# Three-term products of a split-precision linear: the order of the matmuls in a granule, and one wait less

## The chip, the cores and the metric

The kernel runs on one core of a Trainium2 chip. The metric is the time of one execution on the device, in microseconds. Engines by their names in the profile: PE is TensorE (PEld its loads of stationary tiles), DVE is VectorE, ACT is ScalarE, POOL is GpSimd, SP is the engine that issues the weight transfers.

## The reference

A forward pass over 256 tokens with a model width of 2048: two blocks (the first with stick-breaking attention and a gated delta rule, the second with block attention and dilated attention, each followed by a gated feed-forward layer of width 5632), then a block with causal pooling and a state-space mixer. Cut to what matters here, nearly all of the arithmetic is products of a 256-row activation with a large float32 weight:

```python
proj = u @ w_in                                    # 2048 x 7184, 2048 x 6144, 2048 x 4096
u = mixed @ w_out                                  # 2048 x 2048
u = (jax.nn.silu(u @ w_gate) * (u @ w_up)) @ w_down   # 2048 x 5632, twice, and back
```

## The kernel before

**Split products.** Both operands of each such product are split in two numbers of a shorter format (fp32r): x = xh + xl and w = whi + wlo. The result is the sum of three products, xh·whi + xl·whi + xh·wlo, accumulated in float32. The activations are split once for each linear (`xh`, `xl`, and `hTh`, `hTl` for the hidden layer). The weights are split as they arrive.

**Granules.** A linear (`ev_gdn`, `ev_sb`, `ev_z`, `ev_out`, `up0a`, ..., `pg`, 19 of them in this order) is cut in chunks of 512 output columns, and a chunk in granules. A granule is 2 tiles of 128 rows of the weight by 512 columns. There are 948 of them in the kernel, numbered from 0; `s_in` begins with granule 800. The 256 tokens are two tiles (t = 0, 1), so that a granule has 2 (rows j) x 2 (tokens t) x 3 (products) = 12 matmuls of 128x128 by 128x512. The x slice is the stationary operand, the weight slice the moving one. A chunk accumulates in a pair of PSUM banks, one for each t, and successive chunks take the two pairs in turn.

**The ring.** SP brings raw weights, two granules a transfer. For each granule ScalarE copies raw to `whi` (L1020, counted by the semaphore `hi_done`), VectorE subtracts to get `wlo` (L1621, counted by `lo_done`). Both go to one of four places (RING = 4). TensorE counts `used` after the last matmul of a granule, and ScalarE writes the place for granule g only when `used` is at g - 3. SP waits for `lo_done` before it brings the next weights to a raw place:

```python
act.wait_ge(S("used"), g - (RING - 1))                       # ScalarE, L1019
act.activation(whi[:, place % RING], raw_granule(place), ACT.Copy).then_inc(S("hi_done"), 1)
dve.wait_ge(S("hi_done"), g + 1)                             # VectorE, L1620
```

**Order of the other work.** Each engine has one program written out by hand. On TensorE small jobs (transposes, attention, the delta rule, the state-space part) stand between two granules (`aside`). On ScalarE and VectorE they stand between two splits, in one queue with them, so that a split can be late because of what stands before it. At the start of a linear the new activation is transposed on TensorE (L524), and split by ScalarE and VectorE, during the first three granules. The split of the fourth granule's weights stands behind that. In `s_in` VectorE has, for each of 8 column tiles, rotations (`pc<-side,grow`), scans (L2210) and products (`u<-u,grow`), with weight splits between them; TensorE has for each the input products L904 and four output groups L914 to L917, two of them before the second granule after the products, two after. A product of VectorE waits for an earlier output group (`y_part`), because its result goes to one of two places that the group reads.

The function that the change touches stands below, with what calls it. `granules` walks through a linear, and `hidden` does the same for the gate and up products of the feed-forward layer in a loop.

Of the kernel before, what the change touches and what calls it, by code (L numbers as in the profile page):

```python
# [14 lines left out]
P = 128  # L15
TOK = 256
TT = TOK // P
# [99 lines left out]
def build(nc, A, out):  # L117

    ctx = ExitStack()
    with ctx:  # L120
        def sb(name, shape, dt=F32, scope=ctx):
            return scope.enter_context(nc.sbuf_tensor(name, [P] + shape, dt))
# [3 lines left out]
        whi = sb("whi", [RING, 2, CH], F32R)  # L126
        wlo = sb("wlo", [RING, 2, CH], F32R)
# [29 lines left out]
        acc = [ctx.enter_context(nc.psum_tensor(f"acc{i}", [P, CH], F32)) for i in range(4)]  # L157
# [22 lines left out]
        def S(name):  # L180

            if name not in sems:
                sems[name] = ctx.enter_context(nc.semaphore(name))
            return sems[name]
# [193 lines left out]
        def g16(k):  # L378

            return grow[:, 544 + 16 * k:560 + 16 * k]  # L380
# [10 lines left out]
        def unit(t, k):  # L391

            o = UNIT + (8 * t + k) * CH
            return ar[:, o:o + CH].rearrange("p (h n) -> p h n", h=4)
# [52 lines left out]
        def _(pe):  # L447
# [8 lines left out]

            def granule(g, ring, pair, lhs_h, lhs_l, k0, first, last):

                def sweep(x, w, start=False, stop=False):
                    for j in range(2):  # L460
                        for t in range(TT):
                            mm = pe.matmul(acc[2 * pair + t][:], x[:, k0 + j, t * P:t * P + P], w[:, ring, j],  # L462
                                           start=start and j == 0, stop=stop and j == 1)
                    return mm

                pe.wait_ge(S("hi_done"), g + 1)
                sweep(lhs_h, whi, start=first)
                sweep(lhs_l, whi)
                pe.wait_ge(S("lo_done"), g + 1)
                sweep(lhs_h, wlo, stop=last).then_inc(S("used"), 1)  # L470

            def linear(*args):
                for _ in granules(*args):
# [2 lines left out]
            def granules(name, lhs_h, lhs_l, freed, aside=None, first_use=None):  # L476

                per = KTS[name] // 2  # L480
                for c in range(CHUNKS[name]):
                    pair = (CHUNK0[name] + c) % 2
                    for j in range(per):
                        if aside:
                            aside(c, j)
                        if first_use:
                            first_use(c, j)
                        if j == 0:
                            for t in range(TT):
                                claim(acc[2 * pair + t], *freed(c, t))  # L490
                        g = gran(name, c, j)
                        granule(g, g % RING, pair, lhs_h, lhs_l, 2 * j, j == 0, j == per - 1)
                        yield
# [168 lines left out]
            for hg in range(2):  # L662
                for t in range(TT):
                    n = 2 * hg + t

                    for s, (o, ready) in enumerate(((1024, "kT_ready"), (0, "qT_ready"))):
                        b = claim(side[2 * t + s], "kT_done" if s == 0 else "qT_done", n + 1)
                        for k in range(4):
                            c0 = o + (4 * hg + k) * P
                            mm = pe.transpose(b[:, k * P:k * P + P], qkv[:, t, c0:c0 + P], ident)  # L670
                        mm.then_inc(S(ready), 1)
                beside()
                for t in range(TT):

                    b = claim(side[2 * t], "decay_arg", 9 * (2 * hg + t + 1))
                    for k in range(4):
                        c0 = t * 8 + 4 * hg + k
                        mm = pe.matmul(b[:, k * P:k * P + P], g16(GL)[:, c0:c0 + 1].to_broadcast([P, P]), tri_u,
                                       start=True, stop=True)
                    mm.then_inc(S("gb_ready"), 1)  # L680
                beside()
                for t in range(TT):
                    n = 2 * hg + t
# [8 lines left out]
                for t in range(TT):  # L692
                    n = 2 * hg + t
                    pe.wait_ge(S("L_done"), lower(n))
                    b = claim(side[2 * t + 1], "LT_done", n + 1)
                    for k in range(4):
                        mm = pe.transpose(b[:, k * P:k * P + P], unit(t, M_)[:, k], ident)
# [75 lines left out]
            def hidden(name):  # L773
                n0, blocks, g0 = FFB[name], CHUNKS[name] // 2, GRAN0[name]

                def block_of(i, first):
                    for m in range(2):
                        for j in range(8):
                            if m == 0 and j == 2 and not first:
                                pe.wait_ge(S("hTl_done"), 2 * n0 + 2 * i - 2)  # L780
                                turn_hidden(i + (n0 - 1))
                            if j == 0:
                                if first:
                                    for t in range(TT):
                                        claim(acc[2 * m + t], "sg_done", 0)
                                else:
                                    pe.wait_ge(S("hm_done" if m else "sg_done"), 2 * n0 + 2 * i)
                            if first and m == 0 and name[3] == "a":
                                features_use(name, h)(0, j)
                            granule(i * 16 + (g0 + 8 * m + j), j % RING, m, xh, xl, 2 * j, j == 0, j == 7)  # L790

                block_of(0, True)
                with pe.Fori(1, blocks) as i:
                    block_of(i, False)
                for t in range(TT):
                    last_reader[acc[t].name] = (S("sg_done"), 2 * (n0 + blocks))
                    last_reader[acc[2 + t].name] = (S("hm_done"), 2 * (n0 + blocks))
                for b in range(2):
                    last_reader[side[b].name] = (S("hTl_done"), 2 * (n0 + blocks - 1))
# [1622 lines left out]
```

## Time and profile before

| | |
|---|---|
| median of 3 runs | 3032.73 us (3031.87 to 3033.37) |
| profiled execution, its own time | 3031.87 us |
| its span | 3030.1 us |
| TensorE busy | 2924.2 us, 97% |
| TensorE's loads busy | 2403.3 us, 79% |
| VectorE busy | 1731.7 us, 57% |
| ScalarE busy | 1415.6 us, 47% |
| GpSimd busy | 74.0 us, 2% |
| weights and the like moved by DMA | 515.45 MB, mean 170 GB/s |

Read from top to bottom: the execution took its own time, of which the span is the part that the profiler saw between first and last instruction. The busy times are shares of the span. Matmuls are pipelined, so a busy TensorE may still have small waits within; the timeline and the table of waits show these.

### The profile page before, as it was taken

To read this page: it belongs to the slowest core of one execution; us is meant where nothing else is said; L and a number is where in the kernel's file an instruction comes from. 1 tells how busy PE (TensorE), PEld (TensorE's weight loads), DVE (VectorE), ACT (ScalarE), POOL (GpSimd) and SP (SyncE) were. 2 spreads that over 40 slices of the span, in tenths; PEclk is the share of its full clock that TensorE was granted. 3 is DMA by queue.
4 is the path that set the end of the run, shared out by engine and by line. 5 is a ranking of instruction groups with operands and counts; after the bars stand their busy time and mean duration, and the time that the engine had idled before them with its cause. 6 is when DMAs were issued, how large, how long until landed. Compare 5 with 4: busy or idle time off the path is not lost.

```text
span 3030.1 us, 34851 instructions
## 1 busy us (share of the span) xinstructions
PE 2924.2 (97%) x13709; PEld 2403.3 (79%) x13709; DVE 1731.7 (57%) x2222; ACT 1415.6 (47%) x1809; POOL 74.0 (2%) x66
## 2 busy tenths in 40 slices
PE   8999999999999999999999999999999999989998
PEld 7888877788888888878887788888888877556876
DVE  5875655644544454554445545544454569998545
ACT  5543375544444444454446444444444454444444
POOL 0000000000000000000000000000000002210000
PEclk9999999999999999999999999999999999999999
DMA  6532245565555555555552565555655554335443
GB/s 236 176 126 93 89 140 189 179 194 193 181 194 194 194 185 190 193 177 185 188 187 86 175 207 187 190 191 194 194 190 185 194 175 132 98 104 168 172 157 125
DMA packets 255293, 515.45 MB, mean 170 GB/s; under 512 B 8240, under 2 KB 8464, under 8 KB 254144
## 3 DMA queue, kind: packets, MB, share of 16 engines
q1 hardware_dynamic: 252896, 501.61, 50.0%
q0 software_dynamic: 2272, 12.10, 1.2%
q8 instruction: 87, 1.43, 0.2%
q14 instruction: 38, 0.31, 0.0%
HBM read 511.58 MB, written 2.10 MB: 170 GB/s over the span
## 4 chain that ended last, share of the span: by engine, by line
PE 87%; DVE 9%; ACT 2%; issue 2%; DMA 0%; SPq 0%; DVEq 0%; ACTq 0%
PE acc L462 80%; PE side L658 2%; DVE u L1609 2%; DVE u L2210 1%; DVE pc L1609 1%; ACT ar L1009 1%; DVE wlo L1621 1%; DVE ar L1609 1%; PE side L524 1%; PE side L769 1%; PE side L553 1%; DVE ar L1612 0%; ACT whi L1020 0%; DMA raw<-in_ev_w_in 0%; ACT L1009 0%
## 5 line engine op out<-in xcount | busy, mean ns | idle before, releaser
L1621 DVE TENSOR_TENSOR wlo<-raw,whi 128x1024 fp32r<-128x1024 f32 x948 | 1155.3, 1226 | 1114.3 <-ACT whi L1020 1113.5
L1020 ACT ACTIVATE whi<-raw 128x1024 fp32r<-128x1024 f32 x948 | 996.8, 1059 | 1201.3 <-PE acc L462 1199.7
L462 PE MATMUL acc<-whi,xh 128*128 128x512 f32 x3072 | 841.1, 396 | 10.9 <-ACT whi L1020 4.7
L462 PE MATMUL acc<-wlo,xh 128*128 128x512 f32 x3072 | 825.4, 391 | 22.6 <-DVE wlo L1621 22.6
L462 PE MATMUL acc<-whi,xl 128*128 128x512 f32 x3072 | 824.1, 390 | 0.0
L462 PEld LDWEIGHTS acc<-wlo,xh 128*128 128x128 f32 x3072 | 577.6, 188 | 146.7 <-DVE wlo L1621 26.0
L462 PEld LDWEIGHTS acc<-whi,xl 128*128 128x128 f32 x3072 | 578.5, 188 | 122.2
L462 PEld LDWEIGHTS acc<-whi,xh 128*128 128x128 f32 x3072 | 568.9, 189 | 132.7 <-issue 9.6
L462 PE MATMUL acc<-whi,hTh 128*128 128x512 f32 x720 | 194.2, 392 | 2.7 <-ACT u L1009 2.7
L462 PE MATMUL acc<-wlo,hTh 128*128 128x512 f32 x720 | 193.3, 391 | 0.0
L462 PE MATMUL acc<-whi,hTl 128*128 128x512 f32 x720 | 193.3, 390 | 0.0
L462 PEld LDWEIGHTS acc<-whi,hTh 128*128 128x128 f32 x720 | 135.7, 189 | 30.9 <-ACT u L1009 2.9
L462 PEld LDWEIGHTS acc<-wlo,hTh 128*128 128x128 f32 x720 | 135.7, 189 | 28.3
L462 PEld LDWEIGHTS acc<-whi,hTl 128*128 128x128 f32 x720 | 135.7, 189 | 28.3
L658 PE MATMUL side<-ar 128*128 128x128 f32 x720 | 86.6, 277 | 10.1 <-ACT h L1009 6.6
L658 PEld LDWEIGHTS side<-ar 128*128 128x128 f32 x720 | 84.7, 192 | 14.4 <-DVE ar L1609 4.7
L1009 ACT ACTIVATE ar<-side 128x512 f32<-128x512 f32 (+2 forms) x121 | 65.7, 572 | 54.3 <-PE side L553 36.5
L1009 ACT ACTIVATE ar<-ar 128x512 f32<-128x512 f32 (+2 forms) x58 | 31.8, 559 | 101.3 <-DVE ar L1612 82.1
L1009 ACT ACT_TABLE_LOAD x57 | 73.1, 1283 | 12.8 <-DVE cols L1666 6.1
L1609 DVE TENSOR_TENSOR u<-u,grow 128x512 f32<-128x512 f32 x88 | 56.5, 686 | 4.2 <-ACT ar L1009 1.5
L524 PE MATMUL side<-cc,h 128*128 128x128 f32 x192 | 33.0, 338 | 21.3 <-DVE h L1612 18.8
L1009 ACT ACTIVATE ar<-acc,st 128x512 f32<-128x512 f32 x56 | 35.4, 684 | 36.1 <-PE acc L462 34.5
(227 smaller groups left out, 1356.5 us busy)
## 6 DMA issues: line engine op xcount, KB each, us to landing
raw<-in_ffn_w_gate SPq DMA_DIRECT2D x88, 1024.0 KB, 5.1
raw<-in_ffn_w_up SPq DMA_DIRECT2D x88, 1024.0 KB, 5.1
raw<-in_ffn_w_down SPq DMA_DIRECT2D x88, 1024.0 KB, 5.0
raw<-in_ev_w_in SPq DMA_DIRECT2D x56, 1024.0 KB, 5.1
raw<-in_od_w_in SPq DMA_DIRECT2D x48, 1024.0 KB, 5.1
raw<-in_w_in SPq DMA_DIRECT2D x32, 1024.0 KB, 5.3
raw<-in_ev_w_out SPq DMA_DIRECT2D x16, 1024.0 KB, 5.0
raw<-in_od_w_out SPq DMA_DIRECT2D x16, 1024.0 KB, 5.0
```

The lines of the kernel that those rows point to most:

```text
L462: mm = pe.matmul(acc[2 * pair + t][:], x[:, k0 + j, t * P:t * P + P], w[:, ring, j], start=start and j == 0, stop=stop and j == 1)
L524: mm = pe.transpose(b[:, j * TOK + t * P:j * TOK + t * P + P], src[:, t, k * P:k * P + P], ident)
L553: mm = pe.transpose(b[:, jb * TOK + t * P:jb * TOK + t * P + P], pj[:, t, (2 * j + jb) * P:(2 * j + jb + 1) * P], ident)
L658: mm = pe.matmul(bank[:, k * P:k * P + P], lhs(k), rhs(k), start=True, stop=True)
L769: mm = pe.transpose(side[b][:, jb * TOK + t * P:jb * TOK + t * P + P], hm[:, t, (2 * b + jb) * P:(2 * b + jb + 1) * P], ident)
L1009: act.activation(o, i, f, **kw).then_inc(S(done), 1)
L1020: act.activation(whi[:, place % RING], raw_granule(place), ACT.Copy).then_inc(S("hi_done"), 1)
L1609: dve.tensor_tensor(o, a, b, op).then_inc(S(done), 1)
L1621: dve.tensor_tensor(wlo[:, place % RING], raw_granule(place), whi[:, place % RING].bitcast(F32), ALU.subtract).then_inc(S("lo_done"), 1)
L2210: dve.tensor_tensor_scan(x, magnitude(4 * ct + r), x, start(r, m), mult, add)\
```

## The change

Before, a granule went through three sweeps of four matmuls: xh with whi, xl with whi, and then, behind a wait for `lo_done`, xh with wlo. Within a sweep the two banks of the pair alternated. After, the granule waits for `lo_done` at its head (`wlo` is computed from `whi`, so that `hi_done` is implied and its wait is gone), and then makes all three products of one (j, t) in a row, in the order xh·whi, xh·wlo, xl·whi. Three matmuls in a row thus go to one bank, then three to the other. The number of matmuls, their operands, the first and last of an accumulation and the count `used` are as before.

```diff
             def granule(g, ring, pair, lhs_h, lhs_l, k0, first, last):
 
-                def sweep(x, w, start=False, stop=False):
-                    for j in range(2):
-                        for t in range(TT):
-                            mm = pe.matmul(acc[2 * pair + t][:], x[:, k0 + j, t * P:t * P + P], w[:, ring, j],
-                                           start=start and j == 0, stop=stop and j == 1)
-                    return mm
-
-                pe.wait_ge(S("hi_done"), g + 1)
-                sweep(lhs_h, whi, start=first)
-                sweep(lhs_l, whi)
                 pe.wait_ge(S("lo_done"), g + 1)
-                sweep(lhs_h, wlo, stop=last).then_inc(S("used"), 1)
+                for j in range(2):
+                    for t in range(TT):
+                        tok = slice(t * P, t * P + P)
+                        for n, (x, w) in enumerate(((lhs_h, whi), (lhs_h, wlo), (lhs_l, whi))):
+                            mm = pe.matmul(acc[2 * pair + t][:], x[:, k0 + j, tok], w[:, ring, j],
+                                           start=first and j == 0 and n == 0,
+                                           stop=last and j == 1 and n == 2)
+                mm.then_inc(S("used"), 1)
```

## Rows read from the trace of the kernel before

**Rows 1.** The page: busy time, share and count of each engine; granted clock in tenths
```profile
PE 2924.2 (97%) x13709; PEld 2403.3 (79%) x13709; DVE 1731.7 (57%) x2222; ACT 1415.6 (47%) x1809; POOL 74.0 (2%) x66
...
PEclk9999999999999999999999999999999999999999
```

**Rows 2.** The page: the chain that ended last, by engine, shares of the span
```profile
PE 87%; DVE 9%; ACT 2%; issue 2%; DMA 0%; SPq 0%; DVEq 0%; ACTq 0%
```

**Rows 3.** Timeline of a steady stretch: start, length, engine, line, operation, count, idle before
```profile
1005.63 1.07 PE L462 MATMUL acc<-whi,xh 128*128 128x512 f32 x4
...
1008.35 1.07 PE L462 MATMUL acc<-whi,xh 128*128 128x512 f32 x4
1008.55 1.06 ACT L1020 ACTIVATE whi<-raw 128x1024 fp32r<-128x1024 f32 x1 [1.60 <-PE acc L462]
...
1009.64 1.23 DVE L1621 TENSOR_TENSOR wlo<-raw,whi 128x1024 fp32r<-128x1024 f32 x1 [1.43 <-ACT whi L1020]
```

**Rows 4.** Table of waits: who waited for whom, us in total, times, longest
```profile
PE acc L462 <- DVE wlo L1621: 22.6, 8, 3.7
```

**Rows 5.** Timeline of TensorE, first and last of 48 matmuls of L588
```profile
36.90 0.28 PE L588 MATMUL side<-xh,wab_h 128*16 128x256 f32 x1
...
42.41 0.28 PE L588 MATMUL side<-xl,wab_h 128*16 128x256 f32 x1
```

**Rows 6.** Timeline at starts: up0a, od_out, ev_gdn's granule 31, pg
```profile
591.72 3.50 DVE L1621 TENSOR_TENSOR wlo<-raw,whi 128x1024 fp32r<-128x1024 f32 x3
...
592.17 1.07 PE L462 MATMUL acc<-whi,xh 128*128 128x512 f32 x4
...
1642.04 4.63 DVE L1621 TENSOR_TENSOR wlo<-raw,whi 128x1024 fp32r<-128x1024 f32 x4
...
1642.83 1.07 PE L462 MATMUL acc<-whi,xh 128*128 128x512 f32 x4
...
113.92 1.22 DVE L1621 TENSOR_TENSOR wlo<-raw,whi 128x1024 fp32r<-128x1024 f32 x1 [0.19 <-ACT whi L1020]
...
113.94 1.19 PE L462 MATMUL acc<-whi,xh 128*128 128x512 f32 x4
...
2928.79 3.50 DVE L1621 TENSOR_TENSOR wlo<-raw,whi 128x1024 fp32r<-128x1024 f32 x3 [10.33 <-ACT whi L1020]
...
2928.90 1.16 PE L462 MATMUL acc<-whi,xh 128*128 128x512 f32 x4 [2.21 <-ACT whi L1020]
```

**Rows 7.** Timeline around one stall of s_in
```profile
2581.47 1.22 DVE L1621 TENSOR_TENSOR wlo<-raw,whi 128x1024 fp32r<-128x1024 f32 x1
...
2582.75 1.20 PE L462 MATMUL acc<-wlo,xh 128*128 128x512 f32 x4 [1.80 <-DVE wlo L1621]
...
2584.04 0.59 PE L914 MATMUL side<-u,ar 128*32 128x256 f32 x2
...
2584.47 0.59 PE L915 MATMUL side<-u,ar 128*32 128x256 f32 x2
...
2585.02 2.35 DVE L1621 TENSOR_TENSOR wlo<-raw,whi 128x1024 fp32r<-128x1024 f32 x2
...
2587.29 2.49 DVE L1609 TENSOR_TENSOR u<-u,grow 128x512 f32<-128x512 f32 x4
```

**Rows 8.** Timeline of the preparation in s_in
```profile
2520.01 2.77 DVE L1621 TENSOR_TENSOR wlo<-raw,whi 128x1024 fp32r<-128x1024 f32 x2
...
2520.47 1.07 PE L462 MATMUL acc<-whi,xh 128*128 128x512 f32 x4
...
2527.55 1.09 PE L893 MATMUL side<-cc,ar 128*128 128x128 f32 x8 [0.56 <-DVE ar L1609]
```

**Rows 9.** Timeline, a later stall; windows, end of row: PEclk, DMA share, GB/s
```profile
2661.98 2.08 PE L462 MATMUL acc<-wlo,xh 128*128 128x512 f32 x4 [3.70 <-DVE wlo L1621]
...
2667.65 2.50 DVE L1609 TENSOR_TENSOR u<-u,grow 128x512 f32<-128x512 f32 x4 [1.04 <-PE side L917]
...
2643.00:2670.00 27.00, 23.30 (x102) 14.58 (x100) 25.48 (x56) 10.89 (x12) 6.77 (x5) 0.87 0.31 101
```

## The prediction

> **What bounds the kernel now.** I read the page first. TensorE is busy for 97% of the span at a granted clock of nearly full speed, and VectorE for 57% [rows 1]. The chain that ended last runs for 87% on TensorE and 9% on VectorE [rows 2]: outside a few stretches, a microsecond added to TensorE's queue is a microsecond of the end.
>
> Then the timeline of a steady stretch. A granule (12 matmuls) starts at 1005.63 and the next at 1008.35, so a granule takes 2.72 us, 227 ns a matmul; the load of the stationary tile lies under the matmul before it. When the granule ends, ScalarE starts a whi at 1008.55 and VectorE ends the wlo from it at 1009.64 + 1.22 = 1010.86, 2.51 us after the end of that granule [rows 3]. It is for the granule that starts three later (the ring has four places), at 1008.35 + 3 x 2.72 = 1016.5. So in steady state wlo is ready some 5.6 us before its granule even starts. The table of waits agrees: in the whole kernel, the matmuls waited for wlo in 8 places only, 22.6 us together [rows 4].
>
> So the question is where wlo is ready later than the granule's first matmul, though before its ninth. I went through the timeline for that, taking the n-th wlo for the n-th granule. Of 948 granules there are 22 such, in three kinds: the fourth granule at the start of a linear (or one near it, 12 in all), two granules in the preparation of the state-space part, and every fifth granule of s_in's second half (8 of them).
>
> **The change, part by part.**
>
> *Same work.* 12 matmuls a granule before and after, same tiles, same release of the ring place (the count "used" rises after the last of 12), one wait fewer. ScalarE, VectorE and the queues are told nothing new. Cost of the wait that goes: nothing, hi_done is always before lo_done.
>
> *Order of the matmuls.* Three in a row now go to one accumulator bank, where the two banks alternated; and of each three the second has the same stationary tile as the first (3,792 of 11,376). The trace has no 512-column matmuls in such an order. The nearest row is L588: 48 matmuls of 256 columns, all into one bank, from 36.90 to 42.41, 117 ns each [rows 5]. Twice that is 234 ns for 512 columns, against 227. Were the whole difference of 7 ns a price of staying in a bank, 2 of 3 matmuls would pay it: 11,376 x 2/3 x 7 = 53 us. Were it a fixed cost of changing the stationary tile, and were that saved on a repeat, 3,792 x 7 = 27 us would be gained. It is most likely only the fixed part of a shorter matmul (a 16-column stationary tile, too), which fits neither, so I take 0 and keep both ends. The Trainium skill (TensorE: Matmul & The Clock Gate, Step-by-step: what each phase is for) says that a separate load lets one load once and multiply repeatedly. Its section Back-to-back issue gap gives 512/2.4 + 2.5 = 215.8 ns for a matmul by itself, which the 227 ns here don't show; if a repeated tile brought it, the gain by the page would be an estimated 3,792 x 11 = 42 us. But the source asks for a tile anew in each matmul.
>
> *The wait moves eight matmuls forward.* Where wlo is ready in between, TensorE now stands until it is. Restart after such a stand: wlo ends at 2582.69, the matmul starts 0.06 us later, and the first four take 1.20 instead of 1.07 us [rows 7], so some 0.11 us more. Price = end of wlo + 0.06 - start of the granule + 0.11.
>
> Starts of linears [rows 6]:
> - up0a's fourth granule: wlo 591.72 + 1.22 = 592.94, start 592.17: 0.94. The same pattern at od_in, up1a and s_in: 0.97, 0.94, 0.98.
> - od_out's fourth: 1642.04 + 1.22 = 1643.26, start 1642.83: 0.61. Same at ev_out and s_out: 0.61 each.
> - ev_gdn's granule 31: 115.14, start 113.94 (restart already in it): 1.26.
> - pg's first: 2930.01, start 2928.90 (the same): 1.17.
> - ev_gdn's first and fourth granules together: the first stands 1.2 us, but in a stretch at the half clock where it loses only 0.6 us of work; the fourth then lacks 0.4. About 1.0.
>
> Together 3.83 + 1.83 + 1.26 + 1.17 + 1.0 = 9.1 us, in ten places (two more granules with a late wlo are behind one of these and cost nothing more). What is queued behind is all of TensorE's order, its transposes too. TensorE is back to back there, so nothing gives this back before the end.
>
> *s_in, preparation.* The granule that starts at 2520.47 has the first of the two wlo from 2520.01; they take 2.77 us, and with 1.2 for the second the first ends at 2521.6: 2521.6 + 0.06 - 2520.47 + 0.11 = 1.3. But the transposes of L893 soon after waited 0.56 us for VectorE, which gives about half back [rows 8]. 0.7 us is left, and VectorE's first rotation then waits for TensorE's result, so it counts.
>
> *s_in, the eight stalls.* Here VectorE sets the time. Take the one whose wlo is done at T = 2582.69. Before: 4 matmuls are left, L914 starts at T + 1.35, the first output group (8 passes, two of them from 2584.04 to 2584.47, so 0.215 each) is done 1.9 later, at about T + 3.2. VectorE does two products, two wlo (2585.02 + 2.35) and wants that group at T + 4.60 = 2587.29 [rows 7]: 1.3 us to spare. After: 12 matmuls come behind T, L914 at about T + 0.06 + 0.11 + 2.72 + 0.1 = T + 3.0, the group done at T + 4.93. VectorE is 0.33 us late. The eight matmuls that stood before the stall are gone from there, so TensorE's idle lump before the next one stays as it is, some 2 to 4 us. Four stalls at full clock (granules 826, 831, 841, 851): 4 x 0.35 = 1.4.
>
> Three stalls fall into a stretch at the half level (1.2 GHz). The profile shows it: after the idle of 3.70 us at 2661.98 four matmuls took 2.08 us, VectorE waited 1.04 us for L917, and that window has a mean clock of 0.87 [rows 9]. With 12 matmuls instead of 4 in the slow stretch, VectorE is late by 3.1 instead of 1.1 us there: 2.0 more. For the two with a slow stretch half as long (granules 836 and 856) the same working gives 1.45 and 1.8. The last stall has TensorE on the path from there to the end, so all 8 matmuls count: 8 x 0.227 = 1.8. The Trainium skill (the same page, Why this matters for your kernels) warns of idle gaps of TensorE, which bring the slow clock back; the rows agree in that the longest stalls have it, and it would make the sum larger, not smaller, if idle lumps grew.
>
> Sum of s_in: 0.7 + 1.4 + 5.25 + 1.8 = 9.2 us. **Total: 9.1 + 9.2 = 18.3 us.** The profiled execution took 3031.87 us (span 3030.1 and 1.8 around it), 0.9 under the median of 3032.73; so 3050.2 for its like, 3051 for the median. I say 3050.
>
> **Rivals.**
> - *The repeated stationary tile is cheaper (faster).* Against: every matmul in the profile has a load of its own (13,709 of each), and a load (2403.3 us / 13,709 = 175 ns in the mean [rows 1]) is shorter than the matmul that it lies under. It cancels the 18 us from 18.3 / 3,792 = 4.8 ns per repeat. With the 7 ns above: 3050 - 27 = 3023. Chance 0.07.
> - *Staying in one bank costs.* For: nothing but the 7 ns. With them 3050 + 53 = 3103. Against: the output groups of L914 to L917, four matmuls accumulating in one place, run at an even 0.215. Chance 0.05.
> - *Most of it is absorbed.* The starts of linears might be given back where TensorE later waits (attention, or the next boundary). For: TensorE does idle there. Against: those waits follow from results that TensorE's own late work feeds, so they move along. If all ten places were absorbed: 3032.7 + 9 = 3042. If half of s_in too: 3037, no change. Chance of ending within 0.2%: 0.10.
> - *The clock falls more often.* A granule that stands and then begins may find the half level where it found the full one. Four more stalls at about 1.7 each and two starts at 1.7 add 10 us: 3060 to 3065. Chance 0.12.
> - The forecast, 3042 to 3058: 0.66.
>
> **How the numbers follow.** The likeliest case gives 3050. Its own range is 3042 to 3058. Down to the absorbed case and up to the slower clock it becomes 3038 to 3064, which leaves out some 0.17. What a measurement can tell from no change is about 0.2%, 6 us: 3026.7 to 3038.8. Faster: the first rival, 0.07. Same: 0.10. Slower: the rest, 0.83.
>
> **What the profile after would show.** The steady granule still 2.72 us: the order is free. Its matmuls read whi with xh, wlo with xh, whi with xl in turn. Near 592 a wait of TensorE for VectorE's wlo of some 0.8 us, and at the other starts the like; in the table of waits some 10 more places. In s_in VectorE waiting 0.3 us and more for L917 after each stall, where it waited in two or three; a period from stall to stall some 0.35 us longer. It would be wrong if the steady interval is not 227 ns (3.8 ns on each repeat, or 1 ns on all, is 11 to 14 us), or if the clock's row of tenths changes outside s_in.

## The result, and the profile after

| | before | changed |
|---|---|---|
| median | 3032.33 us (4 runs, 3031.87 to 3033.37) | 3060.47 us (4 runs, 3059.07 to 3060.97) |
| ratio to before | | 1.0091, 95% interval 1.0080 to 1.0103 |
| span of the profiled execution | 3030.1 us | 3056.1 us |

The change makes the kernel 28.1 us slower by the medians, 26.0 by the two spans. The forecast was 3050, 18 us slower. The measured time lies inside its wide range (3038 to 3064) and outside that of its likeliest case (3042 to 3058).

The page of the changed kernel, its lines of busy time and of the granted clock, to be read against [rows 1]:

```profile
PE 2929.4 (96%) x13709; PEld 2409.1 (79%) x13709; DVE 1733.2 (57%) x2222; ACT 1417.3 (46%) x1809; POOL 74.0 (2%) x66
...
PEclk9999999999999999999999999999999999989999
```

The work is the same to the instruction: 13,709 matmuls with as many loads, so that no load of a repeated tile was dropped. One digit of the clock fell from 9 to 8, and it lies in s_in.

The timeline of a steady stretch, TensorE alone (each matmul now has a row of its own, since the groups alternate); the first matmul of a granule, the second, the third, and the first of the next granule:

```profile
1012.49 0.39 PE L464 MATMUL acc<-whi,xh 128*128 128x512 f32 x1
1012.72 0.39 PE L464 MATMUL acc<-wlo,xh 128*128 128x512 f32 x1
1012.94 0.39 PE L464 MATMUL acc<-whi,xl 128*128 128x512 f32 x1
...
1015.21 0.39 PE L464 MATMUL acc<-whi,xh 128*128 128x512 f32 x1
```

12 matmuls in 2.72 us, 227 ns each, as in [rows 3]. In the steady stretch the order costs and brings nothing. The table of waits of the changed kernel, beside [rows 4]:

```profile
PE acc L464 <- DVE wlo L1618: 49.3, 19, 5.4
...
DVE u L1606 <- PE side L914: 18.8, 8, 3.1
```

TensorE waits for wlo in 19 places instead of 8. The second row is the new one: VectorE, which sets the time in s_in, waits for TensorE's output groups in 8 places, 18.8 us; the same wait was 1.4 us in 3 places before.

The timeline at up0a's fourth granule, beside the first two of [rows 6]:

```profile
596.19 0.47 PE L464 MATMUL acc<-whi,xh 128*128 128x512 f32 x1 [0.76 <-DVE wlo L1618]
596.50 0.39 PE L464 MATMUL acc<-wlo,xh 128*128 128x512 f32 x1
```

TensorE stands 0.76 us where it stood not at all, and the step to the second matmul is 0.31 instead of 0.23.

The timeline around the stall of granule 831 in s_in, the same one as in [rows 7]:

```profile
2591.09 1.22 DVE L1618 TENSOR_TENSOR wlo<-raw,whi 128x1024 fp32r<-128x1024 f32 x1
...
2592.36 0.80 PE L464 MATMUL acc<-whi,xh 128*128 128x512 f32 x1 [3.81 <-DVE wlo L1618]
2592.95 0.63 PE L464 MATMUL acc<-wlo,xh 128*128 128x512 f32 x1
2593.38 0.63 PE L464 MATMUL acc<-whi,xl 128*128 128x512 f32 x1
...
2596.72 0.62 PE L911 MATMUL side<-u,ar 128*32 128x256 f32 x2
...
2598.68 2.50 DVE L1606 TENSOR_TENSOR u<-u,grow 128x512 f32<-128x512 f32 x4 [1.69 <-PE side L914]
```

Call the end of wlo T (2591.09 + 1.22 = 2592.31). TensorE idled 3.81 us ahead of it instead of 1.80. Then the matmuls come 0.43 us apart, which is the half level: the output groups (L911, which was L914 before) start at T + 4.4 (forecast T + 3.0, before T + 1.35), and VectorE's third product at T + 6.37 (forecast T + 4.93, before T + 4.60). At all eight stalls matmuls came 0.43 us apart, from the first on or, at granule 826, from the third. The windows of the changed kernel for 200 us of s_in, and under it the same length before (the number after POOL's is the granted clock):

```profile
2560.00:2760.00 200.00, 169.39 (x760) 116.56 (x760) 180.07 (x386) 73.35 (x85) 42.03 (x30) 0.90 0.28 90
```

```profile
2550.00:2750.00 200.00, 176.03 (x817) 116.12 (x816) 195.04 (x423) 77.33 (x90) 42.03 (x30) 0.96 0.32 101
```

VectorE did 195 us of work in 200 before, and 180 after: it is held up. The mean clock went from 0.96 to 0.90.

I laid the last matmul of each granule after beside the one before. The delay grows by 1.26 us in the first granules, 1.25 at granule 31, 0.71 at ev_out, 1.04 at up0a, 1.05 at od_in, 0.71 at od_out, 1.05 at up1a, 1.04 at s_in, 0.71 at s_out and 2.86 at pg: 11.7. At six granules at or near boundaries between linears some comes back, 4.0 together. The preparation in s_in adds 0.6, the eight stalls 17.8. Sum: 11.7 - 4.0 + 0.6 + 17.8 = 26.1, and the spans differ by 26.0.

### The profile page after: what moved, and what is told of

Its sections match the earlier page's. It is cut to its first block, busy times and chain, and to the rows that moved or that the text cites. A ratio compares the mean times of both kernels' runs of the same rounds, so it can differ in the third digit from the quotient of the medians.

```text
span 3056.1 us, 34851 instructions
## 1 busy us (share of the span) xinstructions
PE 2929.4 (96%) x13709; PEld 2409.1 (79%) x13709; DVE 1733.2 (57%) x2222; ACT 1417.3 (46%) x1809; POOL 74.0 (2%) x66
## 4 chain that ended last, share of the span: by engine, by line
PE 86%; DVE 9%; ACT 3%; issue 2%; DMA 0%; SPq 0%; DVEq 0%; ACTq 0%
PE acc L464 79%; PE side L655 2%; DVE u L1606 2%; DVE u L2207 1%; DVE pc L1606 1%; DVE wlo L1618 1%; ACT ar L1006 1%; DVE ar L1606 1%; PE side L521 1%; DVE ar L1609 1%; PE side L766 1%; ACT whi L1017 1%; PE side L550 1%; ACT xh L1006 0%; ACT L1006 0%
## 5 line engine op out<-in xcount | busy, mean ns | idle before, releaser
L464 PE MATMUL acc<-whi,xh 128*128 128x512 f32 x3072 | 1220.6, 397 | 55.6 <-DVE wlo L1618 49.3
L464 PE MATMUL acc<-whi,xl 128*128 128x512 f32 x3072 | 1204.4, 392 | 0.0
L464 PE MATMUL acc<-wlo,xh 128*128 128x512 f32 x3072 | 1204.1, 392 | 0.0
L464 PEld LDWEIGHTS acc<-whi,xh 128*128 128x128 f32 x3072 | 582.2, 190 | 187.6 <-DVE wlo L1618 37.3
L464 PE MATMUL acc<-whi,hTh 128*128 128x512 f32 x720 | 281.1, 390 | 2.7 <-ACT u L1006 2.7
L464 PE MATMUL acc<-wlo,hTh 128*128 128x512 f32 x720 | 280.8, 390 | 0.0
L464 PE MATMUL acc<-whi,hTl 128*128 128x512 f32 x720 | 280.8, 390 | 0.0
L464 PEld LDWEIGHTS acc<-wlo,hTh 128*128 128x128 f32 x720 | 135.4, 188 | 28.1
L1606 DVE TENSOR_TENSOR u<-u,grow 128x512 f32<-128x512 f32 x88 | 56.5, 687 | 21.6 <-PE side L914 18.8
L521 PE MATMUL side<-cc,h 128*128 128x128 f32 x192 | 32.4, 330 | 22.2 <-DVE h L1609 18.8
```

The costliest lines, as they stand in the source:

```text
L464: mm = pe.matmul(acc[2 * pair + t][:], x[:, k0 + j, tok], w[:, ring, j], start=first and j == 0 and n == 0, stop=last and j == 1 and n == 2)
L521: mm = pe.transpose(b[:, j * TOK + t * P:j * TOK + t * P + P], src[:, t, k * P:k * P + P], ident)
L1606: dve.tensor_tensor(o, a, b, op).then_inc(S(done), 1)
```

## The experiments

Theory: the wait for wlo is all of the cost, in the places where wlo is late; in s_in the half clock makes it larger. Each run below is set against runs of the kernel before that were made with it; their medians are 3031.71 for the first four runs below, 3032.59 for the one with three stalls and the middle way, and 3032.93 for the others. Rivals: the order of the matmuls; a cost spread over all granules; twelve matmuls behind the wait cost what they cost, whatever the clock; the delay of one stall feeds the next.

**The wait without the order.** Against the kernel before:

```diff
-                pe.wait_ge(S("hi_done"), g + 1)
+                pe.wait_ge(S("lo_done"), g + 1)
                 sweep(lhs_h, whi, start=first)
                 sweep(lhs_l, whi)
-                pe.wait_ge(S("lo_done"), g + 1)
                 sweep(lhs_h, wlo, stop=last).then_inc(S("used"), 1)
```

> The order of before (three sweeps), with the wait for wlo at the head of the granule. It separates the wait from the order of the matmuls. Theory (the wait is the whole cost, the order is free): 3060, as the changed kernel, within 2 us, and a steady granule of 2.72 us. Rival (part of the 28 us comes from staying in one bank or from repeated stationary tiles): 3032 + 28 - that part, so clearly under 3058.

Measured: 3058.73 us, ratio 1.0089 (1.0072 to 1.0106). Its table of waits has the two rows of the changed kernel over again:

```profile
PE acc L462 <- DVE wlo L1620: 50.0, 19, 5.4
...
DVE u L1608 <- PE side L916: 18.7, 8, 3.1
```

So the early wait alone makes the 28 us, within the interval of some 5 us; the unchanged 227 ns of the steady stretch says the same of the order more sharply (1 ns on every matmul would be 11 us).

**The late wait in 21 granules of 948.** `granule` keeps the new order, but for a list, in which the three sweeps and two waits of before stand:

```diff
+OLD_ORDER = {0, 3, 31, 115, 147, 411, 507, 539, 803, 817, 819, 883, 916} | {826 + 5 * k for k in range(8)}
...
+                if isinstance(g, int) and g in OLD_ORDER:
...
+                    return
```

> The changed kernel, with the order and the late wait of before in 21 granules alone: 0, 3, 31, 115, 147, 411, 507, 539, 803, 817, 819, 883, 916, and 826 to 861 in steps of 5. 927 granules keep the new order. Theory (all of the cost sits in the granules whose wlo is late): 3032, within 2 us. Rival (a cost spread over all granules, of the order or of the wait): the 28 us stay for the most part, 3055 and more.

Measured: 3033.11 us, ratio 1.0002 (0.9992 to 1.0011). With 927 granules in the new form the time is that of before, within some 3 us. The cost sits in the 21. The prediction had counted 22: granule 32, whose wlo was late by 0.11 us, stands right behind 31 and kept the new form here.

**The clock in the stalls: 8 and 16 matmuls of filling ahead of the wait.** Added to the changed kernel (the comments are mine):

```diff
+                if isinstance(g, int) and g in STALLED:      # 826, 831, ..., 861
+                    pe.wait_ge(S("hi_done"), g + 1)
+                    for n in range(8):                       # and 16
+                        pe.matmul(acc[2 * pair + n % 2][:], lhs_h[:, k0, n % 2 * P:n % 2 * P + P], whi[:, ring, 0],
+                                  start=first and n < 2, stop=False)
+                    first = False
```

> The changed kernel, with 8 more matmuls (xh with whi, 1.8 us) ahead of the wait in the 8 stalled granules of s_in, so that TensorE's idle lump there is as long as before the change; they add to the accumulator, so the output isn't the reference's. The work behind the wait stays 12 matmuls. Theory (the longer idle lump brings the half clock to all eight stalls, and this makes the excess over the forecast): the half clock at some stalls only, 3050 to 3055. Rival (what counts is only that 12 matmuls come behind the wait): 3060, with VectorE's waits as in the changed kernel.

> As the last, with 16 more matmuls (3.6 us) ahead of the wait in the 8 stalled granules, so that TensorE idles 0.5 to 2.2 us there; output not the reference's. Theory of the clock: no half clock in s_in, VectorE late by 0.3 to 0.4 us a stall: 3032 + 9 for the starts + 0.7 + 2.7 + 1.8, about 3046 to 3048. Rival (12 matmuls behind the wait count whatever the clock): 3060.

Measured: 3053.61 us (1.0069, 1.0052 to 1.0086) with 8, and 3044.45 us (1.0043, 1.0026 to 1.0060) with 16. 128 matmuls more, and 16 us less than the changed kernel. VectorE's wait for the output groups, in the tables of waits of the one and of the other:

```profile
DVE u L1616 <- PE side L924: 11.0, 8, 3.0
```

```profile
DVE u L1616 <- PE side L924: 2.2, 8, 0.3
```

And the windows of the second, same stretch as above:

```profile
2560.00:2760.00 200.00, 194.55 (x936) 136.17 (x931) 194.37 (x415) 76.63 (x91) 42.06 (x30) 1.00 0.31 100
```

At a granted clock of 1.00 VectorE is late by 2.2 / 8 = 0.28 us a stall, with all 12 matmuls behind the wait. That is close to the forecast's 0.33. The other 16.6 us of the 18.8 are the clock's. This goes against the rival that the 12 matmuls count whatever the clock. The time is some 2 us under what I expected for 16.

The run with 8 has both kinds of stall side by side. At granules 831, 841 and 851 all matmuls came at the full clock, and VectorE waited 0.27 to 0.29 us; at the other five they came 0.43 us apart, and it waited 1.7 to 3.0. But the idle ahead of the stall doesn't tell which is which. The first matmul behind the wait at 831 and at 836:

```profile
2595.84 0.50 PE L474 MATMUL acc<-whi,xh 128*128 128x512 f32 x1 [1.75 <-DVE wlo L1628]
```

```profile
2622.57 0.62 PE L474 MATMUL acc<-whi,xh 128*128 128x512 f32 x1 [1.77 <-DVE wlo L1628]
```

The idle is the same, and the second is at the half level. What the three runs show is how often it happens: at all eight stalls with idle lumps of 3.8 to 5.4 us, at five with lumps about as long as before the change (1.8 to 3.6), at none with 0 to 1.8. Why it is these five stays open.

**s_in with the old form, and s_in alone with the new one.** The old form stands in `granule` as above, under the condition `800 <= g < 864` in place of the list, and under its opposite.

> The changed kernel, with the order and late wait of before in the 64 granules of s_in (800 to 863). It prices the ten places outside. Theory: the nine of them that are left (one start lies in s_in) cost 8.1 us by the forecast, and by the changed kernel's trace about as much: 3032 + 8 = 3040. Rival (most of it is absorbed at the boundaries): 3034 or less.

> The kernel before, with the new order and early wait in the 64 granules of s_in alone. By the forecast 3032 + 9.2 + 1.0 for the start that lies in s_in = 3042. By the changed kernel's trace (17.8 for the eight stalls, 0.6 for the preparation, 1.0 for the start): 3051.

Measured: 3041.30 us (1.0029, 1.0019 to 1.0038) and 3048.99 us (1.0051, 1.0035 to 1.0068), against 3032.93. Outside s_in the change costs 8.4 us, within it 16.1. The two sum to 24.5 where the whole has 28.1; with intervals of some 3 and 5 us that is no contradiction, and no exact sum either. Most of the cost of the starts is not absorbed.

**One stall by itself.** Old form in s_in, but for granules 826, 841 and 856.

> The changed kernel, with the order and late wait of before in s_in, but for the three stalled granules 826, 841 and 856. It adds three stalls of the new kind, each alone between stalls of the old kind, to the run with the old order in all of s_in (3041.3). Theory (the idle lump grows because of the eight matmuls that left the front of this very stall): each costs as much as in the changed kernel, a good 2 us, with the half clock at all three: 3047 to 3048. Rival (it grows because of the stall before, whose delay feeds the next one): the three cost 0.35 us each or little more, 3042 to 3043.

Measured: 3050.15 us (1.0054, 1.0037 to 1.0071), 8.8 above the run with the old form in all of s_in (9.2 with each against its own runs of before), so some 3 for each, and 2 us more in all than I expected. In the trace VectorE waited 3.0, 2.7 and 2.7 us behind the three, where it waited 1.9, 2.0 and 3.1 behind the same ones in the changed kernel: all 12 matmuls were at the half level at each of them here. The timeline: the stall of granule 831 (old form, after a new one), that of 841 (new form, after an old one), and VectorE's product after it:

```profile
2594.30 1.77 PE L463 MATMUL acc<-wlo,xh 128*128 128x512 f32 x4 [1.76 <-DVE wlo L1633]
```

```profile
2647.45 0.79 PE L479 MATMUL acc<-whi,xh 128*128 128x512 f32 x1 [4.74 <-DVE wlo L1633]
...
2654.77 2.50 DVE L1621 TENSOR_TENSOR u<-u,grow 128x512 f32<-128x512 f32 x4 [2.70 <-PE side L929]
```

The stall after a costly one idles 1.76 us, about the 1.80 of [rows 7]. The one with the new form idles 4.74 us, though the stall ahead of it is an old one. So the long idle is a matter of this granule's own eight matmuls, and the rival (each stall feeds the next) falls for the idle. Of the clock this can't be said: the four matmuls at 831 took 1.77 us instead of 1.20, the last of them 0.43 apart, after an idle that in the kernel before was followed by the full clock.

**wlo ready in time.** VectorE's split of each stalled granule is moved from behind the scans to ahead of them, in the changed kernel and in the one before. Cut to the place of the move:

```diff
                     if at_ == SSM_AT[ct] + 3:
                         rotate(4 * ct + 3)
+                        split(GRAN0["s_in"] + at_ + 1)
+                        ahead.add(GRAN0["s_in"] + at_ + 1)     # and not again in its own turn
                         scan_tiles(ct)
```

> The changed kernel, with VectorE's split of each of the 8 stalled granules moved ahead of the scans, so that its wlo is ready when TensorE comes to it. Theory (the stall is a matter of where VectorE's queue has the split): the stalls are gone and VectorE waits for output groups no more than before the change: 3032 + 9 to 10 = 3042. Rival (TensorE idles as long elsewhere in the period, the clock falls all the same, and VectorE waits as now): 3050 and more.

> The kernel before, with the same move of VectorE's split. VectorE sets the time in s_in and its work is the same. Theory: it gains at most VectorE's present waits there (1.8 us) and the four matmuls behind the last stall (0.9 us): 3029.5 to 3032, no clear difference. Rival (the stall itself costs TensorE's queue something that the end sees): 3025 or less.

Measured: 3045.38 us (1.0044, 1.0030 to 1.0059) and 3035.45 us (1.0007, 0.9997 to 1.0016), against 3032.93. In the changed kernel the move takes back 15 us: VectorE's wait for the output groups is 0.6 us in the stretch of the eight. The time is 3 us above what I expected. The kernel before gained nothing; its median is 2.5 us higher, which the interval doesn't tell from no change. The waits in s_in of the first show a likely reason, and one thing more:

```profile
DVE wlo L1620 <- ACT whi L1017: 5.8, 7, 0.9
```

```profile
PE side L911 <- DVE u L1606: 25.1, 8, 4.2
```

With its queue rearranged VectorE comes to a later wlo before ScalarE has made the whi for it, 0.8 us a period. The kernel before with the same move has this wait too, 6.2 us in 8 places, and 0.7 in 2 without it. That it makes the 3 us is argued, not tested.

The second row says that TensorE's idle did not go away. It moved from ahead of the stalled granule to behind it, in front of the output groups, where TensorE now waits for VectorE's products. The rival had that half right: the clock still fell, to a mean of 0.93 over 2560 to 2760. But the 12 matmuls no longer lie between wlo and the output groups that VectorE needs, and VectorE hardly waits.

**A middle way: four matmuls ahead of the wait.** Against the changed kernel, the arguments of the matmul left out:

```diff
+                pe.wait_ge(S("hi_done"), g + 1)
+                sweep(lhs_l, whi, start=first)
                 pe.wait_ge(S("lo_done"), g + 1)
                 for j in range(2):
                     for t in range(TT):
                         tok = slice(t * P, t * P + P)
-                        for n, (x, w) in enumerate(((lhs_h, whi), (lhs_h, wlo), (lhs_l, whi))):
+                        for n, w in enumerate((whi, wlo)):      # both with lhs_h
...
```

> A middle way in all granules: the four matmuls of xl with whi first, then the wait for wlo, then xh with whi and xh with wlo in turn (the repeated stationary tile is kept). Eight matmuls behind the wait instead of 12 or 4, and 0.91 us of cover. Theory (a price only where wlo is later than the cover): the starts lack 0.0 to 0.3 us each instead of 0.7 to 1.3, 2 us together; in s_in the output group is done at T + 4.0 at the full clock, which is in time, and 0.5 to 1.7 late where the clock falls: 3036 to 3042. Rival (what the early wait costs does not go with the cover, but comes with any new order): 3050 and more.

Measured: 3041.25 us (1.0027, 1.0018 to 1.0037). The cost goes with the cover: with four matmuls ahead of the wait it is 8.7 us, with none 28. The steps at the starts are 0 to 0.4 us, but for pg's 1.6. Most of what is left is the clock in s_in again (0.92 over 2560 to 2760): VectorE waits 9.1 us for the output groups, 2.0 us at the most.

No version was faster than the kernel before.

## Why the prediction was right, and where it was off

**The order is free**: right. 227 ns a matmul after as before, and the early wait alone gives the changed kernel's time within its interval. Both ends that I kept for it (27 us gained, 53 lost) were far from it. The Trainium skill (TensorE: Matmul & The Clock Gate, Step-by-step: what each phase is for) says that a load once made can serve many matmuls; here each matmul kept its load, and the repeat brought nothing.

**The places**: right. With the old form in 21 of the 22 granules found in the trace the time was 3033.11, against 3031.71 for the kernel before.

**The starts**: forecast 9.1. The steps were 0.61 forecast and 0.71 measured (three places), 0.94 to 0.98 forecast and 1.04 or 1.05 measured (four), 1.26 and 1.25 at granule 31, 1.0 and 1.26 at the first. Only pg was off, 1.17 forecast and 2.86 measured: the matmuls behind its wait came 0.43 us apart there for a while, the half level, after an idle of 3.47 us in place of 2.21. The sum is 11.7, of which 4.0 came back at boundaries, 7.7 net; the run with the old form in s_in gives 8.4 for all but one of these places. I had said that nothing comes back. Where most comes back the profile shows less of the half clock: around the start of s_out, where 1.5 us came back, the mean clock is 0.91 before (2810 to 2830) and 1.00 after (2835 to 2855), and just ahead of pg, where 1.2 did, 0.76 (2912 to 2926) and 0.87 (2938 to 2951). That this is the whole reason is argued, not tested.

**The preparation in s_in**: 0.7 forecast, 0.6 measured.

**The eight stalls**: this is the term that was mis-sized. Forecast 1.4 + 5.25 + 1.8 = 8.5 us, measured 17.8. The step that failed reads: the eight matmuls "are gone from there, so TensorE's idle lump before the next one stays as it is, some 2 to 4 us". I let TensorE carry its delay from one stall to the next, where it would fill the time of the eight matmuls that had moved. The runs showed that the lump grows at every stall. The eight matmuls are missing from its front, 8 x 0.227 = 1.8 us, and at five stalls the lump grew by 1.8 to 2.4 us (2.07 to 4.11 at 826, which has no stall ahead of it, and 1.80 to 3.81 at 831; 2.64 to 4.74 at 841 by itself). At three (836, 846 and 856) it grew by 1.0. The timelines suggest why: TensorE carries a delay only as far as VectorE had time to spare; beyond that VectorE waits for TensorE, both are late by the same, and relative to VectorE TensorE comes to the next stall no later. In the kernel before VectorE had such time, without a wait, behind the stalls just ahead of these three. (It had it behind 826 too, but there TensorE waited 0.76 us for VectorE later in the same period, and that wait went.) With the longer lumps all eight stalls have the half clock where four had it.

The working at the full clock was right (0.33 forecast, 0.28 measured with filling), and that for the long slow stretch too (late by 3.1 forecast, waits of 2.9 to 3.1 measured at the stalls of granules 836, 846 and 856); what was wrong is how many stalls have which. The Trainium skill (the same page, Why this matters for your kernels) tells to avoid longer idle gaps of TensorE between bursts of matmuls. The traces agree for the number of stalls: at the eight lumps of 3.8 us and more of the changed kernel the clock fell, and with 16 matmuls of filling it stayed at 1.00. They do not for each single stall: with 8 matmuls of filling the clock was at the half level at a stall with 1.77 us of idle and full at one with 2.65.

The rival "the clock falls more often" had 0.12 and named 3060 to 3065. It is what happened, with four more stalls and one start (pg), through a mechanism of which the forecast had all pieces and one step wrong. So the likeliest case was wrong by 10 us, and it is this rival's share of the range that holds the measured time.

**Absorbed**: in part, 4.0 of the 11.7 us of the starts, where the rival needed all. **Cheaper repeat, cost of a bank**: neither is seen.

## What to carry to other kernels

When a wait is moved forward on the engine that does most of the work, look through the whole trace for the few places where what it waits for is late; here 21 of 948 granules made the 28 us to within the noise, and the steady state told nothing. Then ask of each such place how long the engine now idles ahead of it: work moved from before a wait to behind it lengthens the idle and the work after it together, and on TensorE the idle can halve the speed of exactly that work. And a delay beyond what the other engine has to spare isn't carried to the next period; it is paid in each.

## What I had not expected of the hardware

More work made the kernel faster than the changed one: 128 matmuls of filling, 29 us of TensorE's time at 227 ns, took 16 us off (3060.5 to 3044.5), since the mean clock over the stretch of the stalls (2560 to 2760) was 1.00 where it was 0.90.
